# First norm taken by halves of its channels, with three projections' first weight chunks multiplied between the halves

## What is computed

```python
mod = silu(c) @ ada_w[0] + ada_b[0]                 # 6 slices of 1024 channels
shift, scale, gate, shift2, scale2, gate2 = split(mod, 6)
h = rms_norm(x, norm1_g[0]) * (1.0 + scale) + shift
proj = h @ w_in[0]                                  # q, k, v, conv input ga with its gate gb, branch gates
...
x = x + gate * (merged @ w_out[0])                  # merged: attention and a 31-tap convolution, gated
```

## Time and profile before

| | |
|---|---|
| time, median of 3 runs | 2455.96 us (2454.06 to 2459.22) |
| time of the profiled execution | 2457.7 us |
| its span, first to last instruction | 2455.5 us |
| PE busy | 2385.3 us, 97% |
| DVE busy | 1935.9 us, 79% |
| ACT busy | 1409.3 us, 57% |
| mean granted TensorE clock | 0.994 of full |

### The profile page before, as it was taken

The page is one execution under the profiler, slowest core; times in us unless marked ns, Lnnn a source line. Parts: engine busy times, 40 slices in busy tenths (PEclk is TensorE's granted clock), DMA queues, the critical chain, the costliest instruction groups (busy, mean ns, idle before and its releaser), DMA issues.

```text
span 2455.5 us, 31642 instructions
## 1 busy us (share of the span) xinstructions
PE 2385.3 (97%) x12811; PEld 2049.2 (83%) x12811; DVE 1935.9 (79%) x1864; ACT 1409.3 (57%) x1402; POOL 17.4 (1%) x33
## 2 busy tenths in 40 slices
PE   5999999999999999999999999999999999999998
PEld 5997888989888899898888978888888888888886
DVE  6998878787786665675445768898989898989897
ACT  2653433545443464364344547777777777777776
POOL 0000000000000000000000000000000000000000
PEclk9999999999999999999999999999999999999999
DMA  9556989435597445455555449999999999999996
GB/s 348 191 178 239 324 313 330 154 130 172 191 356 278 150 138 181 149 195 175 192 184 169 164 148 364 364 362 347 366 348 363 353 365 346 366 349 361 354 363 217
DMA packets 434774, 653.03 MB, mean 266 GB/s; under 512 B 20144, under 2 KB 323888, under 8 KB 434624
## 3 DMA queue, kind: packets, MB, share of 16 engines
q1 hardware_dynamic: 432592, 644.63, 76.1%
q0 software_dynamic: 2032, 6.33, 0.8%
HBM read 649.82 MB, written 1.05 MB: 265 GB/s over the span
## 4 chain that ended last, share of the span: by engine, by line
PE 90%; DVE 6%; ACT 2%; issue 1%; DMA 1%; SPq 0%; ACTq 0%; DVEq 0%
PE pair L2029 27%; PE pair L2031 27%; PE pair L2030 27%; PE pair L2061 2%; PE tb L2259 2%; DVE rest L1140 1%; PE pair L2441 1%; PE pair L2173 1%; PE tb L2133 1%; DMA raw<-in_ada_w 1%; DVE hT L1259 1%; DVE aw L1512 1%; DVE gat L1159 1%; ACT aw L720 0%; PE pair L2187 0%
## 5 line engine op out<-in xcount | busy, mean ns | idle before, releaser
L1140 DVE TENSOR_TENSOR rest<-raw,head 128x2048 fp32r<-128x2048 f32 x542 | 1239.9, 2291 | 288.3 <-ACT head L691 272.7
L691 ACT ACTIVATE head<-raw 128x2048 fp32r<-128x2048 f32 x542 | 1035.6, 1912 | 310.6 <-PE pair L2031 280.5
L2029 PE MATMUL pair<-head,hTh 128*128 128x512 f32 x1664 | 665.7, 400 | 8.0 <-DVE hTl L1214 4.0
L2031 PE MATMUL pair<-head,hTl 128*128 128x512 f32 x1664 | 650.6, 391 | 0.0
L2030 PE MATMUL pair<-rest,hTh 128*128 128x512 f32 x1664 | 649.9, 391 | 0.0
L2029 PEld LDWEIGHTS pair<-head,hTh 128*128 128x128 f32 x1664 | 313.2, 188 | 74.5 <-DVE hTl L1214 5.7
L2031 PEld LDWEIGHTS pair<-head,hTl 128*128 128x128 f32 x1664 | 312.9, 188 | 66.4
L2030 PEld LDWEIGHTS pair<-rest,hTh 128*128 128x128 f32 x1664 | 313.5, 188 | 61.7 <-issue 1.2
L2029 PE MATMUL pair<-hTh,head 128*128 128x256 f32 x1104 | 314.4, 285 | 7.3 <-DVE rest L1140 2.8
L2031 PE MATMUL pair<-hTh,rest 128*128 128x256 f32 x1104 | 312.4, 283 | 0.0
L2030 PE MATMUL pair<-hTl,head 128*128 128x256 f32 x1104 | 312.4, 283 | 0.0
(11 more groups left out here) (309 smaller groups left out, 1785.8 us busy)
## 6 DMA issues: line engine op xcount, KB each, us to landing
raw<-in_moe_w_gate SPq DMA_DIRECT2D x224, 512.0 KB, 5.2
raw<-in_moe_w_up SPq DMA_DIRECT2D x224, 512.0 KB, 7.0
raw<-in_moe_w_down SPq DMA_DIRECT2D x224, 512.0 KB, 5.9
raw<-in_w_in SPq DMA_DIRECT2D x152, 512.0 KB, 4.7
raw<-in_ada_w SPq DMA_DIRECT2D x96, 512.0 KB, 5.6
raw<-in_w_ffn_in SPq DMA_DIRECT2D x88, 512.0 KB, 5.5
raw<-in_w_ffn_out SPq DMA_DIRECT2D x44, 512.0 KB, 5.6
raw<-in_w_out SPq DMA_DIRECT2D x40, 512.0 KB, 4.6
```

The lines of the kernel that those rows point to most:

```text
L691: act.activation(head[:, c.split, :], raw[:, c.raw, :], ACT.Copy).then_inc(heads_done, 1)
L1140: dve.tensor_tensor(rest[:, c.split, :], raw[:, c.raw, :], head[:, c.split, :].bitcast(F32), ALU.subtract).then_inc(rests_done, 1)
L2029: pe.matmul(out_, lh, rh, start=start, stop=False, skip_group_check=True)
L2031: return pe.matmul(out_, ll, rh, start=False, stop=stop, skip_group_check=True)
```

## The change

- The slices (0,0) and (0,1) are loaded by halves of their columns: two chunks of 512 rows by 512 columns for channels 0 to 511 of each, and two for channels 512 to 1023 (`plan_first_mods`). The first 4 MB of the list then hold all that the first half of the norm needs. The other four chunks stand behind the first weight chunks.
- DVE adds a chunk up in four instructions of 512 columns (`first_mod_chunk`), where there were two of 1024. PE sums a half with 4 matmuls.
- DVE copies out channels 0 to 511 with scale and shift as before. ACT copies channels 512 to 1023 from PSUM to `hT` unscaled (two new instructions); DVE scales them in place later.
- PE takes the first chunks of `ga0`, `gb0` and `q0`, with the sums for the second half between them, and then their second chunks (`first_projections`), `keep_busy` with 8 instead of 12. The list of loads is reordered to suit.
- `mod_sum(0,3)` goes from before `k0` to behind it, `mod_take(0,3)` from before the angles to before `rope`.
- As `gb0`'s last chunk is now chunk 4 and not 3, `feed` ahead of `upad*oT` makes rest 6 too.

```diff
+    FIRST = ("ga0", "gb0", "q0")
+
+    def plan_first_mods(j, half):
+
+        for q in range(2):
+            cols = slice(j * D + half * NT, j * D + (half + 1) * NT)
+            plan.seq.append(("m", (j, (half, q)), halves(tiles(mod_weights(0))[:, 4 * q:4 * q + 4, cols], NT)))
...
-            queue_mods((0, 0), (0, 1))
-            plan_mods(8)
+            plan.slices += [(0, 0), (0, 1)]
+            plan_first_mods(0, 0)
+            plan_first_mods(1, 0)
...
+            sources = [column_chunks(w, n0) for n0 in (1536, 2048, 0)]
+            for ch in range(2):
+                for i in range(3):
+                    if ch == 0 and i == 2:
+                        plan_first_mods(0, 1)
+                    if ch == 1 and i == 0:
+                        plan_first_mods(1, 1)
+                    if ch == 1 and i == 2:
+                        plan_mods(2)
+                    plan.weight(sources[i][ch])
+            plan_mods(2)
...
@@ ScalarE, norm_of_input
+                for t in range(T):
+                    act.wait_ge(sem("norm_turned"), 2 * t + 2)
+                    act.activation(hT[:, 4:8, t * P:(t + 1) * P], bank(f"norm0.{t}")[:, 1, :].rearrange("p (k s) -> p k s", s=P),
+                                   ACT.Copy).then_inc(sem("half_copied"), 1)
                 feed(1)
                 for t, half in HALVES_FIRST:
+                    if (t, half) == (0, 1):
+                        feed(3)
                     split(f"norm0.{t}{half}", 4 * half, 4 * half + 4, slice(t * P, (t + 1) * P))
...
@@ VectorE
+            def first_mod_chunk(n):
+
+                _, (j, (half, q)), _ = plan.seq[n]
+                acc = accumulator(j)[:, half * NT:(half + 1) * NT]
+                dve.wait_ge(landed[n % RAW], 32 * (n // RAW + 1))
+                if q > 0:
+                    dve.wait_ge(rests_done, last_mod[0])
+                for r in range(4):
+                    src, c_ = raw[:, n % RAW, r * NT:(r + 1) * NT], cact[:, 4 * q + r:4 * q + r + 1]
+                    if q == 0 and r == 0:
+                        did(dve.tensor_scalar(acc, src, c_, None, ALU.mult))
+                        now()
+                    else:
+                        ins = dve.scalar_tensor_tensor(out=acc, in0=src, scalar=c_, in1=acc, op0=ALU.mult, op1=ALU.add)
...
-                seen[0] = 5
+                seen[0] = 3
                 mods_now()
-                for part in taken:
-                    mod_take(*part)
-                for half in range(2):
-                    for t in range(T):
-                        evac_turned(0, t, half, scale, shift)
-                    if half == 0:
-                        feed(1)
-                    for t in range(T):
-                        rest_turned(0, t, half)
+                for k, j in taken:
+                    mod_take(k, j, 0)
+                for t in range(T):
+                    evac_turned(0, t, 0, scale, shift)
+                for t in range(T):
+                    dve.wait_ge(sem("norm_turned"), 2 * t + 1)
+                    dve.wait_ge(sem("half_copied"), t + 1)
+                    dve.sem_inc(evac["dve"], 1)
+                feed(1)
+                for t in range(T):
+                    rest_turned(0, t, 0)
+                feed(3)
+                mods_now()
+                for k, j in taken:
+                    mod_take(k, j, 1)
+                for t in range(T):
+                    for i in range(4, KD):
+                        part = hT[:, i, t * P:(t + 1) * P]
+                        ins = dve.tensor_scalar(part, part, scale[:, i:i + 1], shift[:, i:i + 1], ALU.mult, ALU.add)
+                        if i < KD - 1:
+                            did(ins)
+                    ins.then_inc(sem("hT_ready"), 1)
+                for t in range(T):
+                    rest_turned(0, t, 1)
...
-            for n in range(5):
+            for n in range(3):
                 mod_chunk(n)
...
@@ TensorE
+            def first_projections():
+
+                for ch in range(2):
+                    for n, name in enumerate(FIRST):
+                        c, ps = At(3 * ch + n), flat4(bank(name))
+                        if ch == 0:
+                            free(name)
+                            if n == 0:
+                                keep_busy(bank(name), 8)
+                        if n == 0:
+                            ready(f"norm0.1{ch}")
+                        pe.wait_ge(rests_done, c.placed())
+                        for k in range(4):
+                            for i in range(4):
+                                wcols = slice(k * NT + i * P, k * NT + (i + 1) * P)
+                                ins = three(ps[:, i, :], head[:, c.split, wcols], rest[:, c.split, wcols], hTh[:, 4 * ch + k, :],
+                                            hTl[:, 4 * ch + k, :], (ch, k) == (0, 0) and i % 2 == 0, (ch, k) == (1, 3))
+                        ins.then_inc(chunk_used, 1)
+                        if ch == 0 and n > 0:
+                            mod_sum(0, n - 1, 1)
```

More of the change, by code:

```diff
@@ L315, in build @@
     for n, (k, j) in enumerate(SLICES):
-        FIRST_PART[k, j] = sum(2 if SLICES[m][1] in (2, 5) else 1 for m in range(n))
+        FIRST_PART[k, j] = sum(2 if SLICES[m][1] in (2, 5) or m < 2 else 1 for m in range(n))
     UNSPLIT = sorted(plan.unsplit)
@@ L546, in mod_part @@
         def mod_part(k, j, part=0):
+            if (k, j) in SLICES[0:2]:
+                return 2 * part + j
             return FIRST_PART[k, j] + part
-        MOD_PARTS = [(k, j, part) for k, j in SLICES for part in range(2 if j in (2, 5) else 1)]
+        MOD_PARTS = sorted(((k, j, part) for n, (k, j) in enumerate(SLICES) for part in range(2 if j in (2, 5) or n < 2 else 1)),
+                           key=lambda part: mod_part(*part))
         def mod_bank(k, j, part):
-            return 0 if (k, j, part) in ((0, 1, 0), (0, 2, 1), (0, 4, 0)) else 1
+            return 0 if (k, j, part) in ((0, 1, 0), (0, 1, 1), (0, 2, 1), (0, 4, 0)) else 1
         def bank_read(k, j, part):
@@ L1141, in make_rest @@
                                   ALU.subtract).then_inc(rests_done, 1)
+            def first_mod_chunk(n):
[9 more added lines that the diff above has]
+                        now()
+                    else:
+                        ins = dve.scalar_tensor_tensor(out=acc, in0=src, scalar=c_, in1=acc, op0=ALU.mult, op1=ALU.add)
+                        if r < 3:
+                            did(ins)
+                            now()
+                ins.then_inc(rests_done, 1)
+                last_mod[0] = freed_by_rests(n)
+                if q == 1:
+                    dve.wait_ge(rests_done, freed_by_rests(n))
+                    dve.sem_inc(sem("acc_ready"), 1)
             def mod_chunk(n):
                 _, (i, q), _ = plan.seq[n]
+                if i < 2:
+                    first_mod_chunk(n)
+                    return
                 k, j = SLICES[i]
@@ L1192, in mod_take @@
                     dve.wait_ge(sem("mod_read"), e + 1)
+                    return
+                if (k, j) in SLICES[0:2]:
+                    cols = slice(4 * part, 4 * part + 4)
+                    ps, b = tb[mod_bank(k, j, part)][:, cols], pcol("ada_b", 8 * j + 4 * part, 4)
+                    dve.tensor_tensor(biased[:, cols] if j else sh[:, cols], ps, b, ALU.add).then_inc(sem("mod_read"), 1)
+                    dve.wait_ge(sem("mod_read"), e + 1)
+                    if j:
+                        did(dve.scalar_tensor_tensor(out=gs[:, cols], in0=biased[:, cols], scalar=1.0, in1=pcol("norm1_g", 4 * part, 4),
+                                                     op0=ALU.add, op1=ALU.mult))
+                        now()
                     return
@@ L1268, in rest_turned @@
                 dve.tensor_tensor(hTl[:, ks, toks], hT[:, ks, toks], hTh[:, ks, toks].bitcast(F32), ALU.subtract).then_inc(htl_ready, 1)
-                if half == 1:
+                if half == 1 and n > 0:
                     dve.sem_inc(evac["dve"], 1)
@@ L2131, in mod_sum @@
                 ps = tb[mod_bank(k, j, part)][:, 0:KD]
-                for i in range(KD):
+                for i in range(4 * part, 4 * part + 4) if (k, j) in SLICES[0:2] else range(KD):
                     ins = pe.matmul(ps[:, i:i + 1], acc[:, i * P:(i + 1) * P], ones[:, 0:1], start=True, stop=True)
@@ L2342, in _ @@
                     mod_sum(0, 1)
[L2343 to L2345 removed]
+                    first_projections()
+                else:
+                    linear("ga1", 512, turn=True, busy=4, splits=("norm2.10", "norm2.11"))
+                    linear("gb1", 512, turn=True)
+                    linear("q1", 512, turn=True)
+                linear(f"k{l}", 512, turn=True)
                 if l == 0:
                     mod_sum(0, 3)
[L2348 removed]
                 rotate(l)
```

29 lines of the change are left out of this document (13 added, 16 removed).

## The result

The changed kernel takes 2464.07 us in the median of 8 runs (2462.59 to 2467.37), beside 2457.3 us of the kernel before in the same sitting (8 runs, 2454.06 to 2459.91): a ratio of 1.0032, with a 95% interval of 1.0022 to 1.0041. It is slower by 0.3%, and 2464.0 was forecast. Measured again in another group of runs the ratio was 1.0037 (1.0023 to 1.0051).

What follows compares the result with a forecast made beforehand. DVE's queue beside PE in layer 0, slack 1.15 us: 9.7 late at `v0`, less 1.15, gives 8.5, or 6.8 without the clock's fall; taking 8.0, 2455.96 + 8.0 = 2464 us, range 2456.5 to 2469.

Steps and rivals of the forecast that it cites:

- What bounds the kernel: Layer 0: PE and DVE run side by side; DVE has 1.15 us to spare, so more lateness delays the program.
- All of it arrives at the end: End of layer 0's mixer: PE is busy 97%, so a delay there delays the program's end by as much.
- Third chunk 0.7 late: Loads at the start: `ada_w` in rows of 2 KB brings the third chunk at 20.8, bounds 0 and 0.9.
- Turning at half clock: PE turning `x` before the first matmul: started cold, 32 passes take 6.8; DVE waits 4.5, first matmul 6.6 earlier.
- Multiply-adds: DVE adding up slices: a 512-column multiply-add costs 0.73 with its successor's wait, half a slice 5.6; bounds 0.64 and 0.80.
- the second wait: DVE between the halves of the norm: it waits 5.2 more for the last half sum, 3.5 without the clock's fall.
- third rival: Added instructions cost more: 28 multiply-adds at 0.80 add 2.0; 2466.5, up to 2469 or 2470 with a second fall; chance 0.12.
- Fall of the clock: PE between the halves, after standing still 3.1: 3.4 at half clock, costing 1.7.
- Second half: After the second takes: eight scalings by 0.2, two `hTl` 1.6, rest 3 2.2; PE on at 65.2 after 6.0 of nothing.
- Tap wait: DVE behind `upad*oT`: the taps wait 2.4 for ACT's tap 0, as rest 6 no longer fills that time.
- (0,3) is the same work: Around `k0` and the rotation: `mod_sum(0,3)` behind `k0` is the same work; rotation ends near 103.4, in time.

Runs made afterwards that it cites:

- e6: Kernel before with slices (0,0) and (0,1) loaded and added up by halves in 512-column instructions, old order kept; ratio 1.0019 to the kernel before.
- e8: Changed kernel with the sum over partitions of slice (0,3) and its take put back in their old places; ratio 1.0046 to the kernel before.
- e5: Kernel before with four more products of 128x1024 on DVE behind rest 7 in layer 0; ratio 1.0018 to the kernel before.
- e9: Changed kernel with the product before rest 6, rest 0 before the first takes, rest 3 before the second, and ACT's heads 0, 1, 3, 4 earlier; ratio 1.0006, 2457.07 us.
- e11: e9 with the second half's scaling given to ACT, rest 4 made meanwhile on DVE, 7 useless matmuls in PE's second stop; ratio 1.0013 to the kernel before.
- e4: Changed kernel with the product before rest 6, rests 3 and 4 before the second takes, rest 0 before the first, their heads earlier; ratio 1.0014 to the kernel before.
- e1: Changed kernel with the product upad*oT put ahead of rest 6 on DVE in layer 0; ratio 1.0022 to the kernel before.
- e7: Changed kernel with PE's two long stops filled with 22 and 28 useless matmuls; ratio 1.0045 to the kernel before.
- e10: Changed kernel with PE's two long stops filled with 14 and 14 useless matmuls; ratio 1.0037 to the kernel before, 2464.54 us.

## Why the prediction was right

The time was forecast within 0.1 us, and that is luck. The forecast was 8.0 on top of 2455.96, the median of three runs; the kernel before came out at 2457.3 in eight, so the difference of the medians is 6.8 (5.4 to 10.1 by the interval of the ratio), and the profiled execution, forecast at 2465.7, took 2462.59. What counts is the ledger.

- *What bounds the kernel.* Held: DVE lost 1.2 of its lateness at the reciprocal in the changed kernel and in all others but e6 and e8, where PE was as late as DVE, as the 1.15 in the earlier trace rows said. PE's early start was worth nothing.
- *All of it arrives at the end.* Held in e5 (5.0 to 5.4 throughout), in part in the changed kernel: from the 8.2 its trace goes to 6.6 at 260, 8.3 at 1300 and 4.0 at 2443, as the falls of the clock lie elsewhere in the two traces, and then the wait of 2.39 near the end, of which the prediction has nothing, makes it 5.3 in the span. That the sum came out near the time is in part this.
- *Third chunk 0.7 late.* Wrong: 20.09, against 20.07. The rate in the window 20 to 30 did fall, from 410 GB/s to 387, not to the 368 that was taken; for three chunks that would be 0.4. In the twelve kernels with rows of 2 KB the chunk came between 19.60 and 21.35, at 20.5 in the mean, in the two without at 20.07 and 20.45: too scattered to tell 0.4 from nothing. The Trainium skill, DMA: Bandwidth & Descriptors, Specifications, asks for 512 B at least for line rate. By this rule the term was nothing; the rates of the two windows do not bear it out, the chunk's arrival doesn't decide it.
- *Turning at half clock.* It came, but the pace doubled at 27.55, before the turning was done (19 passes from 23.38 to 27.50, 15 from 27.50 to 29.03): it took 5.8, not 6.8. The clock column of the windows reads 1.00 here in both kernels, as it does in the first window of the earlier trace rows; that the clock was half is read from the pace alone. DVE waited 3.04, not 4.5, and the first matmul was 8.4 earlier, not 6.6.
- *Multiply-adds.* 0.73 was taken and 0.79 measured: half a slice costs 6.2 (38.65 to 44.87), not 5.6. It made the second wait 3.95 instead of 5.2, and cost nothing itself while the wait covered it. The third rival's 28 multiply-adds are too many for the same reason: 7 of them stand ahead of the third chunk, where DVE waits for loads.
- *Fall of the clock.* It came at the place named (37.79 to 41.20) and cost 1.5, where 1.7 was taken.
- *Second half.* In-place scaling took 2.14 for eight, not 1.6. The rests then waited 1.11 for head 3: ACT makes it only behind the second rounding. That wait was missed, though the kernel before has its like at 50.00. The stop of PE was put at 6.0 and was 7.6; its end, put at 65.2, was at 64.87.
- *Tap wait.* 2.4 forecast, 2.21 measured. Rest 7 ended at 92.1 (92.5 forecast), `v0` started at 105.12 (105.0), `rope` was 9.4 late (9.7), the reciprocal 8.2 (8.5).
- *(0,3) is the same work.* Right for the new order, but what the move saves (1.6 to 1.9, e8) was not seen: without it the forecast's mechanism would have given nearly 10.

So the errors, each 0.2 to 1.8, were of both signs and cancelled, most of them because a wait for a sum took up what the work ahead of it gained or lost. Of the 9.4, counted from 20 us on: DVE waits 10.3 (3.04, 3.95, 1.11, 2.21) where it waited 3.9 before (1.85 and 0.44 in the earlier trace rows, 1.11 for the head at 50.00, and 0.5 for ACT ahead of rest 8), which is 6.4; the six chunks of 512 columns cost 2.6 more, by e6; a second set of takes costs 0.6; and the scaling in place saves 0.5. That makes 9.1; the other 0.3 lies in small gaps between instructions. e9 shows the first part to be a matter of order: with 2.3 of such waits, fewer than the kernel before has, it is 1.4 late. Whether the remaining added work could be taken off DVE without new waits is open; e11 is the only attempt.

## What to carry to other kernels

An engine that starts earlier gains only if the queue that sets the end also comes out earlier: find that queue and its slack first, here 1.2 us of DVE at the scores, and count every wait that a new order puts into it, and in the old order too, so that a wait that was always there is not put down to the change. If a step is cut in halves, each half brings its own round trip between engines; put independent work (a rest, a sum) in front of each wait, and no more than fills it, since e4's surplus rest held up the other engine. Two halved instructions cost more than the whole: 1.58 against 1.32 for a multiply-add here. And follow the lateness to the end of the trace: here the clock took some of it back, and a wait in a part that the change does not touch added to it.

## What the hardware showed beside that

- The granted clock falls behind some stops of PE and not behind others of the same length (3.05 us in the changed kernel and in e1), and it can stay low for long behind a short one: the 10.2 us from 1441.69 shown above come 1.1 us after a stop of 1.29, and the changed kernel has the same stop, to 1448.89, and no fall. Filling both stops kept it full there (e7, e10; in e10 through both windows of the changed kernel's falls), and in e10 it then fell at 89.87 for 6.8 us, where the changed kernel has a fall of 3.4 at 92.41.
- A chunk of 1 MB, third in the list, came within 19.60 and 21.35 us in fourteen profiled executions. That spread alone is larger than some of the effects that were looked for.
- DVE can stand idle 2.4 to 2.6 us at the same instruction of the last norm in twelve kernels and not at all in two others, with nothing in the profile that it waits for.
- A filler matmul of 256 float32 columns takes 0.44 us at full clock: 28 of them, meant for a stop of under 8 us, held PE for 12.35.
